# Weight sums of the Strassen feed-forward pairs on VectorE in place of GpSimd

## What is computed

```
def swiglu(x, w_gu, w_down):
    gate, up = jnp.split(x @ w_gu, 2, axis=-1)
    return (jax.nn.silu(gate) * up) @ w_down
```

## Time and profile before

| | us |
|---|---|
| median of 3 runs | 3339.61 |
| lowest, highest | 3334.99, 3339.66 |
| the profiled execution | 3338.69 |
| its span in the profile | 3336.9 |

### The profile page before, as it was taken

The page is one execution under the profiler, slowest core; times in us unless marked ns, Lnnn a source line. Parts: engine busy times, 40 slices in busy tenths (PEclk is TensorE's granted clock), DMA queues, the critical chain, the costliest instruction groups (busy, mean ns, idle before and its releaser), DMA issues. The chain is left out here.

```text
span 3336.9 us, 51736 instructions
## 1 busy us (share of the span) xinstructions
PE 3292.8 (99%) x20422; PEld 2934.4 (88%) x20422; DVE 2409.7 (72%) x3946; ACT 1688.5 (51%) x3071; POOL 788.6 (24%) x589
## 2 busy tenths in 40 slices
PE   9999999999999999999999999999999999999998
PEld 7999888888889998999888888899998888888998
DVE  7878765766697778777765766697868676649776
ACT  5445453645455445444553644554547374335443
POOL 2433110121044413432110121043500001204431
PEclk9999999999999999999999999999999999999999
DMA  4323433253223332333423263233332222323332
GB/s 140 108 96 115 116 98 86 80 150 91 86 92 99 110 102 85 102 106 114 120 76 117 59 148 101 67 102 103 111 98 92 87 80 70 109 91 95 98 109 83
DMA packets 118561, 332.79 MB, mean 100 GB/s; under 512 B 18984, under 2 KB 21800, under 8 KB 118320
## 3 DMA queue, kind: packets, MB, share of 16 engines
q1 hardware_dynamic: 106352, 308.40, 29.3%
q0 software_dynamic: 11680, 20.56, 3.1%
q10 hardware_dynamic: 288, 0.52, 0.0%
HBM read 306.23 MB, written 4.21 MB: 93 GB/s over the span
## 5 line engine op out<-in xcount | busy, mean ns | idle before, releaser
L1926 DVE TENSOR_TENSOR wl<-raw,wh 128x1024 fp32r<-128x1024 f32 (+2 forms) x633 | 772.4, 1224 | 274.3 <-ACT wh L1343 268.8
L1343 ACT ACTIVATE wh<-raw 128x1024 fp32r<-128x1024 f32 (+2 forms) x637 | 553.1, 875 | 350.7 <-PE PS L820 324.7
L820 PE MATMUL PS<-bh,wh 128*128 128x256 f32 x2520 | 708.2, 281 | 16.8 <-DVE wl L1926 13.3
L820 PE MATMUL PS<-bh,wl 128*128 128x256 f32 x2520 | 703.6, 279 | 0.0
L820 PE MATMUL PS<-bl,wh 128*128 128x256 f32 x2520 | 703.5, 279 | 0.0
L820 PE MATMUL PS<-uh,wh 128*128 128x512 f32 (+2 forms) x1656 | 613.9, 371 | 10.4 <-DVE ul L1963 3.5
L820 PE MATMUL PS<-ul,wh 128*128 128x512 f32 (+2 forms) x1656 | 599.4, 362 | 0.0
L820 PE MATMUL PS<-uh,wl 128*128 128x512 f32 (+2 forms) x1656 | 599.2, 362 | 0.0
L820 PEld LDWEIGHTS PS<-bh,wh 128*128 128x128 f32 x2520 | 473.2, 188 | 24.9 <-DVE wl L1926 18.2
L820 PEld LDWEIGHTS PS<-bl,wh 128*128 128x128 f32 x2520 | 479.4, 190 | 0.0
L820 PEld LDWEIGHTS PS<-bh,wl 128*128 128x128 f32 x2520 | 473.3, 188 | 0.6
(11 more groups left out here) (268 smaller groups left out, 5693.0 us busy)
## 6 DMA issues: line engine op xcount, KB each, us to landing
raw<-in_gu SPq DMA_DIRECT2D x218, 512.0 KB, 3.2
raw<-in_win SPq DMA_DIRECT2D x139, 512.0 KB, 3.3
raw<-in_dn SPq DMA_DIRECT2D x80, 320.0 KB, 3.0
raw<-in_dn SPq DMA_DIRECT2D x40, 512.0 KB, 3.7
raw<-in_wbr SPq DMA_DIRECT2D x72, 256.0 KB, 2.6
raw<-in_wout SPq DMA_DIRECT2D x24, 512.0 KB, 3.2
raw<-in_dn SPq DMA_DIRECT2D x40, 256.0 KB, 2.7
raw<-in_wv SPq DMA_DIRECT2D x20, 512.0 KB, 3.4
```

The costliest lines, as they stand in the source:

```text
L820: return e.matmul(out, lhs, rhs, start=start, stop=stop, skip_group_check=True)
L1343: return e.activation(out, in_, f, scale=scale, **more)
L1926: tt(lo, src, hi, SUB).then_inc(*S.lo.up(("lo", c)))
```

## The change

VectorE makes the four sums of every pair but the first of each run (f = 4, 10 and 15), whose sums GpSimd goes on making. In VectorE's iteration f the sums of pair f+1 stand behind `low_g`, behind the low part of c+3, ahead of the second gate and behind the next pair's c+1. The last iteration of a run has none. GpSimd's sums of an opening pair now also wait for VectorE's last sum of the pair before. A raw tile is free again when VectorE's (or GpSimd's) last sum of its pair is done.

```
             if kind in ("sums12", "sums43"):
                 s = 1024 if kind == "sums43" else 0
-                return ws[:, s:s + 1024], (S.pl, kind, p)
+                return ws[:, s:s + 1024], summed(kind, p)
...
-            return [(S.lo, "lo", c), (S.pl, "sums43", CUTS[c][1])]
+            return [(S.lo, "lo", c), summed("sums43", CUTS[c][1])]
+
+        OPENING = {CUTS[j.first][1] for j in JOBS.values() if j.kind == "pair" and (j.tag[2] == PLAIN or j.tag[2] - 1 in PART_AT)}
+
+        def summed(kind, p):
+
+            return (S.pl if p in OPENING else S.dn), kind, p
...
+                def sum_of_weights(f, i):
+
+                    p = CUTS[JOBS["pair", v, f].first][1]
+                    x, y = raw[:, p % 4, :], raw[:, (p + 1) % 4, :]
+                    if i in (1, 3):
+                        E.wait_ge(S.lo, "lo", JOBS["pair", v, f - 1].first + (i + 1) // 2)
+                    if i == 1:
+                        E.wait_ge(S.raw[(p + 1) % 4], "raw", p + 1)
+                        tt(ws[:, 0:512], y[:, 0:512], y[:, 512:1024], ADD).then_inc(*S.dn.up(("sum1", p)))
+                    elif i == 2:
+                        E.wait_ge(S.raw[p % 4], "raw", p)
+                        E.wait_ge(S.dn, "sum1", p)
+                        tt(ws[:, 512:1024], ws[:, 0:512], x[:, 0:512], SUB).then_inc(*S.dn.up(("sums12", p)))
+                    elif i == 3:
+                        tt(ws[:, 1536:2048], x[:, 0:512], y[:, 0:512], SUB).then_inc(*S.dn.up(("sum3", p)))
+                    else:
+                        E.wait_ge(S.dn, "sums12", p)
+                        tt(ws[:, 1024:1536], x[:, 512:1024], ws[:, 512:1024], SUB).then_inc(*S.dn.up(("sums43", p)))
...
                     ahead(c + 2)
                     if not skip:
                         low_g(f - 1)
+                    follows = f + 1 < FT and f not in PART_AT
+                    if follows:
+                        sum_of_weights(f + 1, 1)
                     ahead(c + 3)
                     if f == PLAIN:
                         low_operand(6)
+                    if follows:
+                        sum_of_weights(f + 1, 2)
                     first_gate(f)
                     ahead(c + 4)
+                    if follows:
+                        sum_of_weights(f + 1, 3)
                     second_gate(f)
                     ahead(c + 5)
+                    if follows:
+                        sum_of_weights(f + 1, 4)
...
                     if f > PLAIN:
                         E.wait_ge(S.lo, "lo", JOBS["pair", v, f - 1].first + (1 if which == 12 else 2))
+                        E.wait_ge(S.dn, "sums43", CUTS[JOBS["pair", v, f - 1].first][1])
...
-                sums(PLAIN, 12)
-                sums(PLAIN, 43)
-                for f in range(PLAIN + 1, FT):
+                for f in (PLAIN, *(f + 1 for f in PART_AT if f > PLAIN)):
                     sums(f, 12)
                     sums(f, 43)
```

## The result

| | before | after |
|---|---|---|
| median, us | 3338.52 (4 runs) | 3321.31 (4 runs) |
| lowest to highest | 3334.99 to 3339.66 | 3320.34 to 3321.68 |
| the profiled execution, and its span | 3338.69, 3336.9 | 3321.68, 3319.8 |

The account below looks back on a forecast made before the run. VectorE's loop, stretched by GpSimd's sums, was taken as the bound; without the stretch TensorE's 9.89 us pairs bind. 905.98 - 890.5 = 15.5 us off 3338.69 gives 3323.2, or 3324.1 as median; range 3309 to 3334.

Parts of the forecast that it names:

- What bounds the kernel: VectorE's loop in the pairs, stretched by GpSimd's sums: 10.20 us now, 9.09 with four sums of 0.61, against TensorE's 9.89.
- The order on VectorE: Layout of one pair's instructions from TensorE's start T: no sum delays what TensorE needs, 0.6 us to spare.
- The first pair of a stage: Operand 6, for which product 7 waits, is ready at about 84.4, 2 us ahead; the 0.65 us gap goes.
- The pace: TensorE's matmuls turn to 113 ns only after a gap; without gaps every pair takes 9.89 us.
- rival A: TensorE's fast pace stays: 90 x 9.52 = 856.8 us, 49.2 less than now, 3290.4 us; chance 0.06.
- The sum: All 90 pairs at 9.894 us give 890.5 against 905.98: 15.5 us less.
- B: VectorE exposes whole instruction durations: loop 10.17 us, 0.28 over TensorE per pair; 3329 us; chance 0.04.
- C: Cross-engine waits in VectorE's loop eat the spare, 1.1 us a pair: about 10.2 again, 3333 to 3346 us; chance 0.10.
- D: VectorE's sums take 1.71 us, stretched by two f32 inputs beside DMA writes: about 3590 us; chance 0.06.
- list of kinds: Lengths of the 15 runs of pairs: four of five runs of five 49.47 us, six 61.7, seven 69.1, the last 71.1.

Follow-up runs that it names:

- the run with the small matmul: Changed kernel plus one 64-column matmul ahead of product 4 in the first pair of each run; 3292.55 us, repeated at 3292.78 us.
- the run with one more instruction: Changed kernel plus one 128x512 subtraction per iteration on VectorE, behind sum 3, into a tile nobody reads; 3325.26 us.
- the run with the wait: Changed kernel, but in each run's first pair product 7 also waits for the low half of the next pair's first sum cut; 3323.56 us.

## Why the prediction was right

**What bounds the kernel**, step by step. VectorE's loop was forecast at 9.09 us. In pair 5 of the first stage, where it runs without idle time, the gates' first addition starts at 89.02 and the next pair's at 98.10 in the changed kernel's timeline of VectorE: 9.08. In steady pairs it is 9.89 with 0.60 idle. Of the 0.2 between, 0.14 lies in starts that are farther apart (8.61 us from the first addition to sum 4, against 8.47 in pair 5), the most of it before two low halves that come right behind ScalarE's high halves; the rest is the end of sum 4, which no following instruction overlaps. The price of a sum, 0.61 from start to start, was taken from another instruction of the same form, and held.

**The order on VectorE** came out as laid out: sum 2 was forecast at T+4.58 and starts at 4.57, sum 4 at T+8.87 and starts at 8.81 (1131.80 and 1136.04 less 1127.23). No sum waited for a landing.

**The first pair of a stage**: operand 6 was forecast ready at 84.4; it starts at 83.14 and takes 1.22 us. Its gap is gone.

**The pace**: all 90 pairs at 9.89, pairs 9 and 21 included, which were at 9.52 before. Without that step the forecast would have been wrong by 34 us: it is the 890.5 - 856.8 between the forecast and rival A. Rival A's price was about right (856.8, and 860.97 in the run with the small matmul), and its condition not met.

**The sum**: 15.5 us forecast, 15.6 us measured in the pairs. The other 1.6 us of the medians' 17.2 lie in the scatter of the rest of the kernel.

**The rivals.** B, whole durations: out by the run with one more instruction. C, handoffs that eat the spare: they take 0.14 us a pair, where it needed 1.1. D, stretched sums: they are stretched, to 1.78 us, when GpSimd reads beside them, and then the kernel is 165 us slower than before, the lower clock included; with GpSimd idle they are not. So the price of D exists, but not by D's cause: beside the DMA writes alone every sum takes 0.68 to 0.69 us, and it needs GpSimd's reads to stretch it.

**Where the forecast's reason fell short**: it said that TensorE gets its 113 ns pace "only after such a gap". A gap is neither needed (the 64-column matmul makes none) nor enough (the runs of five in the run with the wait), and the trace of the kernel before already had cases against it: the three stretches above, and the run of five of its first stage, whose last pair takes 9.89 behind gaps of 0.52 and 0.57 us. That run takes 51.22 us and the first stage's run of seven 69.85, which the prediction's list of kinds left out. The number held because all 90 pairs stayed at the pace with which a run starts; that they would was right, but the reason given for it was too simple, and in this one step the forecast had some luck. The run with one more instruction shows how little it takes: there four pairs became partly fast without a gap.

What stays open: why 64 columns ahead of product 4 switch and ahead of product 1 do not, and why the same gap of 0.55 us switched in runs of seven and not in runs of five. Open too is what made the clock fall behind three of five equal gaps. It was not tried whether other widths or places save the 0.28 us that the opening pairs still lose, nor whether the 256-column matmuls of other stages can be switched.

## What to carry to other kernels

When an engine's loop is full, look at whether its instructions are longer than the same ones elsewhere in the trace: moving work onto the full engine can shorten its loop if that takes away what stretches it, here 3.55 us of stretch for 2.44 us of work. Count loops from start to start, not by durations. And look at the distance of matmul starts as well as at gaps: a stream without any gap can still be 4% slower than it need be.

## What the runs showed of the hardware

- VectorE's two-input operations and GpSimd's two-input operations on SBUF hold each other up: on VectorE 1.22 us becomes up to 2.33 and 0.69 up to 1.79, on GpSimd the second sum has a median of 1.30 us in the changed kernel and of 1.63 in the one before. GpSimd memsets of 0.53 us do nothing to VectorE.
- A gapless stream of weight loads and 256-column matmuls has two stable spacings at the same granted clock of 1.00, 113 and 118 ns (9.52 and 9.89 us for 84). Every run of the changed kernel starts in the slow one behind 512-column matmuls and keeps it. Where low halves came late, the stream went over to the other one in either direction, behind a gap of 0.4 us or with none; one 64-column matmul per run is worth 860.97 against 890.40 us.
- Where GpSimd's reads made TensorE wait 10 us in a run of six pairs (73.18 long, 62.61 busy), the granted clock was 0.98, against 1.00 in every stretch of the changed kernel. Behind a single gap of 2.00 us in a full stream it fell to 0.50 in three of five stages, and 12 matmuls took 2.56 us in place of 1.41.
